# 31 instead of 14 seven-product slabs in the FFN down products of a two-block fp32 kernel

## The reference

```
def swiglu(x, w_gate, w_up, w_down):
    return (jax.nn.silu(x @ w_gate) * (x @ w_up)) @ w_down

x = layer_norm(alpha * x + 0.5 * swiglu(...))      # first block, D_FF = 2816
h = h + 0.5 * _swiglu(_rmsnorm(h, ...), ...)       # second block
```

## Time and profile before

| | |
|---|---|
| median of 3 runs | 1590.94 us |
| the profiled execution's own time | 1590.62 us |
| its span, first to last instruction | 1588.9 us |
| TensorE busy | 1581.3 us, 100% |
| VectorE busy | 1138.0 us, 72% |
| ScalarE busy | 831.8 us, 52% |
| 176 loads of gate and up weights, 132 of down weights | 512 KB each, 4.8 and 4.1 us to landing |

### The profile page before, as it was taken

How to read it: one execution, slowest core, us unless ns; L and a number is a source line. 1 busy time by engine, 2 the same in 40 slices (tenths; PEclk the granted TensorE clock), 3 DMA queues, 4 the chain that set the end, 5 groups by cost and what they waited for, 6 DMA issues and landing times.

```text
span 1588.9 us, 21336 instructions
## 1 busy us (share of the span) xinstructions
PE 1581.3 (100%) x8746; PEld 1360.9 (86%) x8746; DVE 1138.0 (72%) x1384; ACT 831.8 (52%) x1125; POOL 35.5 (2%) x53
## 2 busy tenths in 40 slices
PE   9999999999999999999999999999999999999999
PEld 7888898878888888888899888889888888888887
DVE  6678856798767777768757677877766557766785
ACT  5555354775455535555444555556555436545552
POOL 0000000000000000000000000001000011000000
PEclk9999999999999999999999999999999999999999
DMA  9555684445566456655465655657565551056643
GB/s 308 187 197 187 198 270 151 137 139 180 164 206 226 171 199 196 192 183 213 158 225 176 196 185 172 236 176 250 175 188 199 187 199 58 25 167 193 193 154 117
DMA packets 228385, 291.23 MB, mean 183 GB/s; under 512 B 10628, under 2 KB 203840, under 8 KB 228160
## 3 DMA queue, kind: packets, MB, share of 16 engines
q1 hardware_dynamic: 228016, 289.61, 55.0%
q10 hardware_dynamic: 272, 0.26, 0.0%
HBM read 288.78 MB, written 1.05 MB: 182 GB/s over the span
## 4 chain that ended last, share of the span: by engine, by line
PE 95%; DVE 3%; ACT 1%; DMA 0%; POOL 0%; issue 0%; SPq 0%; DVEq 0%
PE bank L2204 24%; PE bank L2209 13%; PE bank L1990 7%; PE bank L1995 7%; PE bank L1999 7%; PE bank L2081 6%; PE bank L2073 6%; PE bank L2068 6%; PE bank L2042 2%; PE bank L2049 2%; PE bank L2044 2%; PE bank L2322 1%; PE bank L2319 1%; PE bank L2317 1%; PE bank L2640 1%; PE bank L1960 1%
## 5 line engine op out<-in xcount | busy, mean ns | idle before, releaser
L1230 DVE TENSOR_TENSOR w_lo<-raw,w_hi 128x2048 fp32r<-128x2048 f32 (+1 forms) x281 | 623.8, 2245 | 93.5 <-ACT w_hi L779 90.4
L779 ACT ACTIVATE w_hi<-raw 128x2048 fp32r<-128x2048 f32 (+1 forms) x280 | 524.8, 1884 | 155.4 <-DVE raw L1218 52.9
L2204 PE MATMUL bank<-xT,w_hi 128*128 128x512 f32 x1664 | 397.3, 391 | 0.0
L2204 PEld LDWEIGHTS bank<-xT,w_hi 128*128 128x128 f32 x1664 | 306.2, 188 | 59.5
L2209 PEld LDWEIGHTS bank<-xT,w_lo 128*128 128x128 f32 x1664 | 213.3, 191 | 8.1
L2209 PE MATMUL bank<-xT,w_lo 128*128 128x256 f32 x1664 | 215.9, 283 | 0.0
L1161 ACT ACTIVATE silu<-bank 128x256 f32<-128x256 f32 x104 | 34.3, 381 | 193.6 <-PE bank L2209 193.6
L2068 PE MATMUL bank<-w_hi,xT 128*128 128x512 f32 (+2 forms) x448 | 117.7, 392 | 0.0
L2081 PE MATMUL bank<-w_lo,xT 128*128 128x512 f32 (+2 forms) x456 | 115.3, 384 | 0.1
L2073 PE MATMUL bank<-w_hi,xT 128*128 128x512 f32 (+2 forms) x448 | 114.4, 384 | 0.0
L1995 PE MATMUL bank<-w_hi,hT_lo 128*128 128x512 f32 x416 | 107.3, 390 | 0.0
(11 more groups left out here) (325 smaller groups left out, 1820.7 us busy)
## 6 DMA issues: line engine op xcount, KB each, us to landing
raw<-in_ffn_w_gate_up_dram SPq DMA_DIRECT2D x176, 512.0 KB, 4.8
raw<-in_ffn_w_down_dram SPq DMA_DIRECT2D x132, 512.0 KB, 4.1
raw<-in_w_in_dram SPq DMA_DIRECT2D x44, 512.0 KB, 4.9
raw<-in_ffn_w_gate_dram SPq DMA_DIRECT2D x42, 512.0 KB, 4.1
raw<-in_ffn_w_up_dram SPq DMA_DIRECT2D x42, 512.0 KB, 5.1
raw<-in_conv_w_in_dram SPq DMA_DIRECT2D x24, 512.0 KB, 4.7
raw<-in_kv_w_dram SPq DMA_DIRECT2D x12, 512.0 KB, 4.8
raw<-in_w_out_dram SPq DMA_DIRECT2D x8, 512.0 KB, 3.7
```

Source lines behind the costliest of these rows:

```text
L779: nc.scalar.activation(w_hi[:, slot, 0:width], raw[:, slot, 0:width], ACT.Copy).then_inc(high_ready, 1)
L1230: nc.vector.tensor_tensor(w_lo[:, slot, 0:width], raw[:, slot, 0:width], w_hi[:, slot, 0:width].bitcast(F32), ALU.subtract).then_inc(low_r ...
L2204: nc.tensor.matmul(o[:], hi[:, c, at], x, start=kh == 0 and c == 0, stop=False, skip_group_check=True)
```

## The change

`SEVEN` names six down slabs (3 to 8) in layers 0, 3, 5 and 9, five (3 to 7) in layer 2 and two (3, 4) in layer 7: 31 in all. `PAIRED` sets how many plain slabs stand ahead of each seven, so the order with six is 0, 3, 4, 1, 5, 6, 7, 8, 2, 9, 10. There the sums of the fifth and sixth seven, and in layer 7 all, live in the memory of `z_sb`. At a layer's end both engines split up to the last slab of the layer before the joins. VectorE signals after the first half of a slab's block sums, and ScalarE makes the high part of the sums in two halves of 1024 columns.

```diff
-SEVEN = {0: (3, 5, 7), 2: (3, 5), 3: (3, 5, 7), 5: (3, 5, 7), 9: (3, 5, 7)}
+SEVEN = {0: (3, 4, 5, 6, 7, 8), 2: (3, 4, 5, 6, 7), 3: (3, 4, 5, 6, 7, 8), 5: (3, 4, 5, 6, 7, 8), 7: (3, 4), 9: (3, 4, 5, 6, 7, 8)}
+PAIRED = (0, 0, 1, 1, 1, 1)
...
+        z_raw, = layer_memory([("z_raw", [P, 2, 4, P], F32)])
+        z_lo, z_hi = layer_memory([("z_lo", [P, 2, 4, P], F32R), ("z_hi", [P, 2, 4, P], F32R)])
         z_sb = sb("z_sb", [P, NT, D])
...
+        def sums_place(n, i):
+            if behind_kv(n):
+                return z_raw[:, i], z_lo[:, i], z_hi[:, i]
+            if i < 4:
+                return s_raw[:, i], s_lo[:, i], s_hi[:, i]
+            return z_raw[:, i - 4], z_lo[:, i - 4], z_hi[:, i - 4]
...
-            for d in sevens(n):
-                order += [plain.pop(0), d]
+            for i, d in enumerate(sevens(n)):
+                if len(order) - i <= PAIRED[i]:
+                    order.append(plain.pop(0))
+                order.append(d)
             return order + plain
...
                 if k in SUMS_OF:
-                    act.wait_ge(b_sums, SUMS_OF[k] + 1)
-                else:
-                    act.wait_ge(arrived[slot], 32 * loads_to(k))
+                    act.wait_ge(b_sums, 2 * SUMS_OF[k] + 1)
+                    nc.scalar.activation(w_hi[:, slot, 0:1024], raw[:, slot, 0:1024], ACT.Copy)
+                    act.wait_ge(b_sums, 2 * SUMS_OF[k] + 2)
+                    nc.scalar.activation(w_hi[:, slot, 1024:SLAB], raw[:, slot, 1024:SLAB], ACT.Copy).then_inc(high_ready, 1)
+                    return
...
                     if sevens(n):
-                        split_to(first_slab[n + 1] - 2)
+                        split_to(first_slab[n + 1] - 1)
                         act.wait_ge(slab_used, last_seven(n))
...
-                step(nc.vector.tensor_tensor(made[:, 0:2, :], b[:, 0:3:2, :], b[:, 3:4, :].to_broadcast([P, 2, 512]), ALU.subtract))
+                nc.vector.tensor_tensor(made[:, 0:2, :], b[:, 0:3:2, :], b[:, 3:4, :].to_broadcast([P, 2, 512]), ALU.subtract).then_inc(b_sums, 1)
+                dve.wait_ge(b_sums, 2 * SUMS_OF[k + 1] + 1)
...
                     if sevens(n):
-                        split_to(first_slab[n + 1] - 2)
-                        dve.wait_ge(slab_used, last_seven(n))
+                        split_to(first_slab[n + 1] - 1)
                         shared_products(n, 0.5)
```

More of the change, by code:

```diff
@@ L119, in two_block_kernel @@
             ("tmp", [P, 512], F32), ("o_norm", [P, 2, S], F32)])
-        n_seven = max(map(len, SEVEN.values()))
-        _, s_raw = layer_memory([("s_raw_pad", [P, 96], F32), ("s_raw", [P, n_seven, 4, P], F32)])
-        _, s_lo, s_hi = layer_memory([("s_pad", [P, 96], F32), ("s_lo", [P, n_seven, 4, P], F32R), ("s_hi", [P, n_seven, 4, P], F32R)])
+        _, s_raw = layer_memory([("s_raw_pad", [P, 96], F32), ("s_raw", [P, 4, 4, P], F32)])
+        _, s_lo, s_hi = layer_memory([("s_pad", [P, 96], F32), ("s_lo", [P, 4, 4, P], F32R), ("s_hi", [P, 4, 4, P], F32R)])
         P1, P5, P6, P7 = bank[0], bank[5], bank[1], bank[4]
+        def sums_place(n, i):
[4 more added lines that the diff above has]
+            return z_raw[:, i - 4], z_lo[:, i - 4], z_hi[:, i - 4]
         ms_of = [o_norm[:, 0, :], gain[:, 2, 0:S]]
@@ L775, in split @@
                 if k in SUMS_OF:
-                    act.wait_ge(b_sums, SUMS_OF[k] + 1)
-                else:
-                    act.wait_ge(arrived[slot], 32 * loads_to(k))
+                    act.wait_ge(b_sums, 2 * SUMS_OF[k] + 1)
[3 more added lines that the diff above has]
+                    return
+                act.wait_ge(arrived[slot], 32 * loads_to(k))
                 nc.scalar.activation(w_hi[:, slot, 0:width], raw[:, slot, 0:width], ACT.Copy).then_inc(high_ready, 1)
@@ L1156, in feature_tile @@
                             act.wait_ge(s_made, seven_before[n] + i + 1)
-                            nc.scalar.activation(s_hi[:, i], s_raw[:, i], ACT.Copy).then_inc(s_high, 1)
+                            s, _, hi = sums_place(n, i)
+                            nc.scalar.activation(hi, s, ACT.Copy).then_inc(s_high, 1)
                         act.wait_ge(slab_used, s0 + 2 * j + 2)
@@ L1227, in split @@
                 if k in BLOCKS_OF:
-                    dve.wait_ge(b_sums, SUMS_OF[k + 1] + 1)
+                    dve.wait_ge(b_sums, 2 * SUMS_OF[k + 1] + 2)
                 dve.wait_ge(high_ready, k + 1)
@@ L1289, in shared_products @@
                 step(onto(rest, p1.unsqueeze(1).to_broadcast([P, 2, 512])))
-                nc.vector.scalar_tensor_tensor(out=right, in0=P5[:].unsqueeze(1).to_broadcast([P, 2, 512]), scalar=-1.0 if has_ln(n) else -factor,
-                                               in1=right, op0=ALU.mult, op1=ALU.add)
+                step(nc.vector.scalar_tensor_tensor(out=right, in0=P5[:].unsqueeze(1).to_broadcast([P, 2, 512]),
+                                                    scalar=-1.0 if has_ln(n) else -factor, in1=right, op0=ALU.mult, op1=ALU.add))
             def layer_norm(n, tt, factor):
@@ L1890, in feature_tile @@
                             dve.wait_ge(s_high, seven_before[n] + i + 1)
-                            nc.vector.tensor_tensor(s_lo[:, i], s_raw[:, i], s_hi[:, i].bitcast(F32), ALU.subtract).then_inc(s_ready, 1)
+                            s, lo, hi = sums_place(n, i)
+                            nc.vector.tensor_tensor(lo, s, hi.bitcast(F32), ALU.subtract).then_inc(s_ready, 1)
                         split_to(s0 + 2 * j + 1 + LEAD)
                     def token_sums(j):
-                        s, a = s_raw[:, sevens(n).index(j)], [[h[:, c, tt * P:(tt + 1) * P] for c in range(2)] for tt in range(NT)]
+                        s, _, _ = sums_place(n, sevens(n).index(j))
+                        a = [[h[:, c, tt * P:(tt + 1) * P] for c in range(2)] for tt in range(NT)]
                         dve.wait_ge(h_ready, 2 * FT * f + 2 * j + 2)
+                        if behind_kv(n) or sevens(n).index(j) >= 4:
+                            dve.wait_ge(xT_ready, 4 * (inputs_before(n) + 1))
                         nc.vector.tensor_tensor(s[:, 2, :], a[0][0], a[1][0], ALU.subtract)
@@ L2305, in combined @@
                         def combined(m):
-                            return s_hi[:, i, m, :], s_lo[:, i, m, :]
+                            _, lo, hi = sums_place(n, i)
+                            return hi[:, m, :], lo[:, m, :]
                         own = [(P1, tokens(0, 0), 0), (Y[0][0], tokens(1, 0), 1), (Y[0][1], combined(3), 2)]
```

## The result

| | before | after |
|---|---|---|
| median | 1590.86 us (4 runs, 1590.77 to 1591.03) | 1618.10 us (4 runs, 1614.99 to 1618.91) |
| profiled execution, span | 1590.62, 1588.9 us | 1618.63, 1616.9 us |
| mean granted clock | 1.000 | 0.992 |

The change made the kernel slower: ratio 1.0167, 95% interval 1.0154 to 1.0180, +27.2 us between the medians. The forecast was 1611 (+20), its range 1604 to 1619.

A forecast was written before the change was run, and what follows sets the result against it. TensorE's instruction list bounds the kernel, VectorE second. Layers 3 and 5 at +4.6 each, 0 +7.7, 2 +4.1, 7 -1.4, 9 +0.7 sum to +20.3 us: 1590.62 becomes 1610.9, median 1611; 8-in-10 range 1604 to 1619.

The forecast's parts named there:

- main case: Whole kernel: VectorE late at four layer boundaries, TensorE waits, clock cost taken as 0; 1611 us, 1605 to 1616, 65%.
- TensorE's saving: Down products: 17 more seven-product slabs, each three matmuls of 0.227 us fewer, take 11.6 us off TensorE's list.
- VectorE's price: Down product: a seven costs VectorE 6.6 us (sums, own low part, low part of sums) against 4.76 on TensorE.
- The start of VectorE's list: VectorE starts slab 25's work 5.86 us after the down product's start T, left as before the change.
- VectorE's room: Layer 3's down product before the change: VectorE idles 3.38 us just before the first addition and little elsewhere.
- The feature tiles: FFN's first half, tiles 3 to 8: an additional low part fits VectorE's idle time, 0.4 us left; cost 0.
- The sum without the clock: Down-product stages of layers 0, 2, 3, 5, 7 and 9 together: +20.3 us, with no cost for the clock.
- The clock: TensorE's clock after boundary waits: bounds 0 and +10 us, taken as 0 as nearest to the rows.
- the second rival: The clock falls in TensorE's waits of 4 to 7 us: up to 1621 us, halfway 1616; 17%.
- The joins: Layer's tail: joins of shared products ahead of the last low parts would have cost another 5 us.
- The halves: ScalarE's high part of the sums in two halves removes VectorE's 0.19 us wait: 0.2 us a seven, no more.
- The other side (hidden, 1579): Down product: VectorE's added work stays covered, only TensorE's list counts, 1579 us; needs at most 5.3 us a seven; 5%.

The follow-up runs named there:

- experiment 1: The changed kernel plus filler matmuls of constants where TensorE waits for the next layer's input at the ends of layers 0, 2, 3, 5: 1610.65 us, ratio 1.0124.
- Experiment 4: The changed kernel with the joins of the shared products again ahead of the layer's last low part on VectorE: 1616.88 us, ratio 1.0163.
- Experiment 6: The changed kernel, 31 sevens, with the last two block sums and the low part of the sums replaced by copies (not the reference's arithmetic): 1594.63 us, ratio 1.0024.
- experiment 3: The changed kernel with 22 sevens in place of 31, the added ones late in the order: 1602.45 us, ratio 1.0072.

## Why the prediction was right, and where not

- **The total: inside the range, outside the main case.** 1618.1 lies 7.1 us above the forecast of 1611. It is outside the 1605 to 1616 of the forecast's own case and 0.9 us inside the range for 8 in 10 (1604 to 1619). The prediction had named this as one of the ways of being wrong (boundary waits there, total off by more than 5 us: the clock or the next layers), and it is the clock.
- **TensorE's saving and VectorE's price: right.** 51 matmuls less. A seven takes 6.58 us on VectorE against 6.6 forecast; low parts are late in sevens 7 and 8 and the next input at four boundaries, as said, and no wait names a transfer.
- **The start of VectorE's list: off by 0.4.** It was left at T + 5.86 and is T + 5.43: the shorter waits for ScalarE (before the last tile's product 0.54 us where it was 1.29) give more back than the added low part takes. So everything behind it comes 0.4 us sooner than forecast: waits of 0.43 and 1.53 in place of 0.9 and 1.8, addition at T + 56.7 in place of 57.1, turnings at 63.6, 60.7, 60.5 and 60.5 in place of 64.0, 61.0, 60.9 and 60.9.
- **VectorE's room: read too small.** That VectorE idles "just before the addition" and "little elsewhere" overlooks a wait for a high part in the trace of before; in layer 2 such waits come to 6.2 us:

```profile
754.21 2.29 DVE L1230 TENSOR_TENSOR w_lo<-raw,w_hi 128x2048 fp32r<-128x2048 f32 x1 [1.87 <-ACT w_hi L779]
```

  The sum is untouched, since it was made from VectorE's list and not from the room. But this kind of idle time is what decides between the two orders with 22 sevens: in layer 3 it was 3.71 us, and 1.10 for a slot, with the sevens late, and 0.45 with the sevens early.
- **The feature tiles: right.** 0.41 us of idle time is left before the tile where there were 1.01, and 0.4 was forecast.
- **The sum without the clock: right.** With the clock held, experiment 1 gives 8.84, 3.81, 4.39, 4.40, -1.34 and 0.50, in all +20.6, against +20.3, with 1.4 us of clock left in layer 0. Its median of 1610.65 stands beside the forecast of 1611; without those 1.4 us it would be some 1.7 below, so that near a match is in part luck.
- **The clock: the term that was mis-sized.** "I take 0, which is nearest to the rows" put the likeliest case on the wrong side. The rows of before held no wait above 1.2 us, so they spoke neither for nor against. The bounds 0 to +10 were right, the price is 8.5 us, and the second rival (up to 1621, halfway 1616) is what happened. The Trainium skill, "TensorE: Matmul & The Clock Gate", section "HAM oscillation — how this bites in real kernels", has just this mechanism (a wait for data, then a group that starts cold); by that rule the trace agrees, with 0.50 behind 6.45 us and 1.00 behind 1.5 us. With the upper bound of +10 the forecast would have been 1621, with half of it 1616. I gave it 17%, which was too little.
- **The joins: wrong.** "The joins in front would have cost another 5" took the wait in the tail as an addition in each layer. Experiment 4 shows it in place of the wait at the turning in layers 0 and 2. In layers 3 and 5 the turning comes 2.6 and 1.4 us later, by the clock, and layer 9 loses 3.4 us; against after the time is 1.2 us lower, against the kernel with the clock held 5 us higher in all, not in each layer.
- **The halves: nearly right.** 0.2 us a seven was forecast, 0.28 measured with 31 sevens.
- **The other side (hidden, 1579): right to put at 5%.** Experiment 6 missed it even at 4.79 us a seven. The bound that the prediction gave for it ("at most 5.3 us on VectorE") was not enough: VectorE waits 3.5 to 4.6 us for the tail's loads then.

## What to carry to other kernels

Price an edit that moves work from the bounding engine to a covered one at the point where the two meet, by the covered engine's list up to there: its room in layer 3 was 3.4 us ahead of the addition, 2.9 behind it and 1.9 in the tail, one added seven costs 4.4, and putting it early instead of late decided between 0.9962 and 1.0072 of the time for the same 22. A wait put on TensorE has a second price in the clock; where the trace of before has no such wait, that is unknown and not zero. Matmuls put into a wait that can't be avoided gave back 7.1 us of 8.5 here.

## What the runs showed of the hardware

- **Shorter waits lowered the clock too.** In experiment 3, the turning after waits of 4.75, 2.69, 1.40 and 2.45 us (layers 0, 2, 3, 5), by stretch as above:

```profile
192.30:197.00 4.70, 4.68 (x18) 3.89 (x19) 2.56 (x4) 2.56 (x3) 0.00 (x0) 0.64 0.00 0
602.40:606.00 3.60, 3.57 (x13) 3.20 (x14) 2.02 (x3) 2.16 (x3) 0.00 (x0) 0.56 0.34 116
788.00:792.00 4.00, 3.88 (x20) 3.18 (x21) 3.22 (x6) 1.61 (x3) 0.00 (x0) 1.00 0.56 179
1066.00:1070.00 4.00, 3.99 (x15) 3.22 (x15) 2.00 (x3) 1.19 (x2) 0.00 (x0) 0.57 0.28 95
```

  The wait of 2.45 us is followed by 0.57, that of 1.40 us by 1.00. The length of the wait alone does not decide. In experiment 1, behind 1.69 us in layer 0, the clock was 0.50 from 197 to 200; in experiment 4 it stayed at 1.00 behind 1.75 us in layer 0, and behind a wait of 3.03 us in layer 9's tail, where the same wait in layer 3 was followed by 0.53:

```profile
1602.30:1606.00 3.70, 3.68 (x16) 3.05 (x17) 1.29 (x2) 0.00 (x0) 0.00 (x0) 1.00 0.10 38
```

  What else decides is not shown here. A matmul group at the low level took 1.88 times as long from start to start (1.71 against 0.91 us in layer 0).
- **A copy is worth half a subtraction on VectorE.** In experiment 6 the copy of 128 x 2048 took 1.22 us where the two-input subtraction of the same size takes 2.29. The Trainium skill, "VectorE: DVE Perf Modes", section "Mode 2×_2P — use both read ports for one tensor", gives a one-input operation in fp32 within SBUF two results in each cycle, and one with two inputs one; the trace agrees, with 1.22 against 2.29.
